# MoBA heads with stationary values and eight row buffers, difference heads with two steps scored early

## The reference

```
# MoBA (8 heads of 64): with 512 tokens and blocks of 256, the top-3 choice of earlier blocks
# takes every earlier block, so each head is causal softmax attention with a linear bias
s = q @ k.T * scale - slope * dist           # 128 rows x (128, 256, 384 or 512) keys per row tile
o = softmax(s) @ v
z = concatenate([o_nsa, o_moba]) @ w_out

# heads with differences (4 heads, two maps m of 64 each, values of 128), no causal mask
p = softmax(q_m @ k_m.T * scale - slope * |dist|)     # m = 0, 1
o = (p[0] - lam * p[1]) @ v
o = rms(o, subln) * 0.8 * silu(gate)
```

## Time and profile before

| | us |
|---|---|
| median of three runs | 1905.12 |
| profiled execution, device time | 1898.13 |
| its span | 1896.2 |
| PE busy in it | 1795.2 (95%) |
| DVE busy | 686.3 (36%) |
| ACT busy | 388.5 (20%) |

### The profile page before, as it was taken

How to read it: one execution, slowest core, us unless ns; L and a number is a source line. 1 busy time by engine, 2 the same in 40 slices (tenths; PEclk the granted TensorE clock), 3 DMA queues, 4 the chain that set the end, 5 groups by cost and what they waited for, 6 DMA issues and landing times.

```text
span 1896.2 us, 32235 instructions
## 1 busy us (share of the span) xinstructions
PE 1795.2 (95%) x13254; PEld 844.1 (45%) x13254; DVE 686.3 (36%) x1747; ACT 388.5 (20%) x910; POOL 139.2 (7%) x209
## 2 busy tenths in 40 slices
PE   5999999999999999999999989999999889989999
PEld 3567657746333332333233323333333274656854
DVE  3469775513223222232322213231313143296140
ACT  2127521602111111111111111011111022261110
POOL 2020000000010011001101101011010100000000
PEclk9999999997999999999999999999999999999999
DMA  9912231422999999999999999999999792100001
GB/s 322 296 45 90 90 107 47 185 78 100 338 386 395 402 405 400 405 387 401 399 402 401 401 404 399 405 390 388 406 402 414 291 309 67 45 1 1 1 0 45
DMA packets 133403, 495.25 MB, mean 261 GB/s; under 512 B 22587, under 2 KB 72677, under 8 KB 84104
## 3 DMA queue, kind: packets, MB, share of 16 engines
q1 hardware_dynamic: 116624, 466.91, 63.3%
q0 software_dynamic: 11264, 19.27, 4.3%
q10 hardware_dynamic: 5368, 7.00, 1.0%
HBM read 481.08 MB, written 17.43 MB: 263 GB/s over the span
## 4 chain that ended last, share of the span: by engine, by line
PE 69%; DMA 20%; DVE 7%; issue 2%; ACT 1%; SPq 1%; POOL 0%; ACTq 0%; DVEq 0%; POOLq 0%
PE bank L1593 22%; DMA ring<-in_exp_w_dram 18%; PE bank L1616 11%; PE bank L437 10%; PE bank L450 8%; PE bank L857 6%; DVE arena L720 2%; PE bank L639 1%; DVE arena L689 1%; DVE arena L805 1%; PE bank L1581 1%; PE bank L412 1%; DMA arena<-in_x_dram 1%; SPq L990 1%; PE bank L1566 1%
## 5 line engine op out<-in xcount | busy, mean ns | idle before, releaser
L1593 PE MATMUL bank<-ring,arena 128*32 128x512 f32 x5568 | 638.1, 599 | 28.4 <-DMA ring<-in_exp_w_dram 19.2
L1593 PEld LDWEIGHTS bank<-ring,arena 128*32 128x32 f32 x5568 | 170.2, 110 | 381.6 <-issue 329.9
L1616 PE MATMUL bank<-ring,arena 128*32 128x512 f32 (+1 forms) x3392 | 309.6, 518 | 16.9 <-DMA ring<-in_exp_w_dram 15.6
L1616 PEld LDWEIGHTS bank<-ring,arena 128*32 128x32 f32 x3392 | 109.7, 110 | 219.1 <-issue 172.5
L437 PE MATMUL bank<-hT,ring 128*128 128x512 f32 x448 | 201.5, 600 | 2.0 <-ACT hT L840 1.1
L1298 ACT ACTIVATE arena<-bank,mod,small 128x96 f32<-128x96 f32 (+2 forms) x256 | 87.4, 423 | 545.2 <-PE bank L1581 545.2
L2060 DVE COPY arena<-bank 128x8 f32<-128x8 f32 (+1 forms) x32 | 5.3, 164 | 363.1 <-PE bank L1566 353.2
L437 PEld LDWEIGHTS bank<-hT,ring 128*128 128x128 f32 x448 | 84.1, 191 | 101.3 <-issue 98.5
L450 PE MATMUL bank<-ring,hT 128*128 128x256 f32 (+1 forms) x640 | 128.2, 360 | 0.0
L2074 DVE TENSOR_TENSOR arena<-bank,arena 128x512 f32<-128x512 f32 x87 | 54.9, 683 | 189.1 <-PE bank L1593 189.1
L450 PEld LDWEIGHTS bank<-ring,hT 128*128 128x128 f32 x640 | 111.4, 190 | 15.2 <-issue 2.4
(11 more groups left out here) (405 smaller groups left out, 1517.6 us busy)
## 6 DMA issues: line engine op xcount, KB each, us to landing
ring<-in_exp_w_dram SPq DMA_DIRECT2D x384, 1024.0 KB, 27.5
ring<-in_ada_w_dram SPq DMA_DIRECT2D x24, 1024.0 KB, 11.8
ring<-in_w_in_dram SPq DMA_DIRECT2D x23, 1024.0 KB, 11.9
ring<-in_w_out_dram SPq DMA_DIRECT2D x8, 1024.0 KB, 5.1
arena<-in_x_dram ACTq DMA_DIRECT2D x1, 2048.0 KB, 17.2
ring<-in_w_in_dram SPq DMA_DIRECT2D x8, 256.0 KB, 5.1
expert_sums<-arena POOLq DMA_DIRECT2D x4, 512.0 KB, 4.2
h_rows<-arena ACTq DMA_DIRECT2D x4, 512.0 KB, 2.6
```

The costliest lines, as they stand in the source:

```text
L1593: mm = pe.matmul(bank[g][QUAD * c:QUAD * (c + 1), :].rearrange("p (h n) -> p h n", h=2), rowsT[:, k, QUAD * g:QUAD * (g + 1)], w[:, :, SW ...
L1616: mm = pe.matmul(bank[b][QUAD * c:QUAD * (c + 1), 0:width], rowsT[:, g, 2 * q + j, :], w[:, col:col + width], start=(q == 0 and j == 0), s ...
```

## The change

MoBA. Eight row buffers instead of three. The probabilities are divided by their row sum on DVE over the whole width before they are transposed. Both heads of a pair get a buffer of turned probabilities of their own (`pair_pT`, keys on partitions, all 512 queries along the row), which ACT fills step by step. When the eight steps of a pair of heads are turned, PE multiplies with 64 columns of values stationary and the turned probabilities moving, 512, 384, 256 and 128 columns wide, the two heads on the two halves of one bank. The result comes out with features on partitions, as `w_out` needs it, and DVE copies it to `hT` in one instruction. The transposes of the NSA half of `omix` move between the first MoBA scores; those of the MoBA half are gone. PE transposes three pairs behind the scores.

Heads with differences. The scores, minima and exps of the first two steps are placed behind the last gate job but one. The PSUM banks are dealt out anew so that this is possible. On DVE the second map gets the factor -lambda * sum0 / sum1 and is added to the unscaled first map; the division by sum0 is applied to the 128-wide result.

```diff
+        moba_p = [work[:, n, :] for n in range(4)] + [omix[:, n, 0:S] for n in range(4)]
+        pair_pT = [omix[:, :, 512:1024], room(6144, [NT, S])]
...
+        def pe_moba(pe):
...
+            def turn(st):
+                n = st["at"]
+                pe.wait_ge(p_ok, n - O_NSA + 1)
+                pe.wait_ge(t_ok, n - 1)
+                for b in range(st["blocks"]):
+                    mm = pe.transpose(bank[4 + n % 2][:, b * P:(b + 1) * P], st["p"][:, b * P:(b + 1) * P], ident[:, :])
+                mm.then_inc(t_done, 1)
+
+            def values(t):
+                pe.wait_ge(t_ok, O_NSA + PAIR * (t + 1))
+                if t >= 2:
+                    pe.wait_ge(o_acc, O_NSA + PAIR * (t - 1))
+                for b in range(NT):
+                    for h in range(2):
+                        lanes = slice(HD * h, HD * (h + 1))
+                        mm = pe.matmul(bank[6 + t % 2][lanes, P * b:S], vtok[:, b, P * t + HD * h:P * t + HD * (h + 1)],
+                                       pair_pT[h][:, b, P * b:S], start=(b == 0), stop=(b == NT - 1), skip_group_check=True)
+                mm.then_inc(o_done, PAIR)
+            pairs = len(moba_steps) // 2
+            for m in range(pairs + LATER):
+                if m < pairs:
+                    scores(moba_steps[2 * m], moba_steps[2 * m + 1])
+                if m < 2:
+                    mixed_turned(pe, 2 * m)
+                    mixed_turned(pe, 2 * m + 1)
+                if m >= LATER:
+                    turn(moba_steps[2 * (m - LATER)])
+                    turn(moba_steps[2 * (m - LATER) + 1])
+                    if m >= LATER + NT and (m - LATER) % NT == 0:
+                        values((m - LATER) // NT - 1)
+            values(pairs // NT - 1)
...
+            def copy(st):
+                n, i, k = st["at"], st["i"], st["at"] - O_NSA
+                act.wait_ge(t_done, n + 1)
+                if k >= PAIR:
+                    act.wait_ge(o_done, O_NSA + PAIR * (k // PAIR))
+                act.activation(pair_pT[st["half"]][:, 0:i + 1, P * i:P * (i + 1)],
+                               bank[4 + n % 2][:, 0:P * (i + 1)].rearrange("p (b q) -> p b q", q=P), ACT.Copy).then_inc(t_ok, 1)
...
+                if m in (0, 2):
+                    mixed(m)
+                    mixed(m + 1)
...
+            def over_sum(st):
...
+                dve.wait_ge(s_exp, n + 1)
+                link(dve.reciprocal(c, ls[:, n % 4:n % 4 + 1]))
+                dve.tensor_scalar(st["p"][:, 0:w], st["p"][:, 0:w], c, None, ALU.mult).then_inc(p_ok, 1)
+
+            def take(t):
+                dve.wait_ge(o_done, O_NSA + PAIR * (t + 1))
+                dve.tensor_copy(hT[:, 4 + t, :], bank[6 + t % 2][:, :]).then_inc(o_acc, PAIR)
...
-                link(dve.reciprocal(c, ls[:, n % 4:n % 4 + 2]))
-                dve.tensor_tensor(c[:, 1:2], lam[:, 5:6], c[:, 1:2], ALU.mult)
-                link(dve.tensor_scalar(p0, p0, c[:, 0:1], None, ALU.mult))
-                dve.scalar_tensor_tensor(out=p0, in0=p1, scalar=c[:, 1:2], in1=p0, op0=ALU.mult, op1=ALU.add)\
-                   .then_inc(w_ok, 1)
+                dve.reciprocal(over, ls[:, n % 4:n % 4 + 1])
+                link(dve.reciprocal(c, ls[:, n % 4 + 1:n % 4 + 2]))
+                link(dve.scalar_tensor_tensor(out=c, in0=c, scalar=lam[:, 5:6], in1=ls[:, n % 4:n % 4 + 1], op0=ALU.mult,
+                                              op1=ALU.mult))
+                dve.scalar_tensor_tensor(out=p0, in0=p1, scalar=c, in1=p0, op0=ALU.mult, op1=ALU.add).then_inc(w_ok, 1)
...
-                dve.tensor_copy(st["dst"], bank[6 + st["at"] % 2][:, 0:P]).then_inc(o_acc, 1)
+                dve.tensor_scalar(st["dst"], bank[1 + st["at"] % 2][:, 0:P], da_over[:, j % 4:j % 4 + 1], None, ALU.mult)\
+                   .then_inc(o_acc, 1)
...
+            act_project(act, link, da_jobs, {da_jobs[-2]["at"]: first_exps})
...
+            dve_project(dve, link, da_jobs, {da_values[1]["at"]: normed, da_jobs[-2]["at"]: first_minima})
```

More of the change, by code:

```diff
@@ L591, in two_block_layer @@
                     bias=bias8[:, h, S - P * (i + 1):S], blocks=i + 1,
-                    over=None, dst=omix[:, i, 512 + HD * h:512 + HD * h + HD], add=False))
+                    i=i, half=h % 2))
         for h in range(4):
@@ L726, in dve_attend, with mixed_turned @@
                     accumulate(steps[m - 3])
-        def pe_da(pe):
[L730 to L735, removed]
+        PAIR = 2 * NT
+        LATER = 3
+        def mixed_turned(pe, t):
+            if t >= 2:
+                pe.wait_ge(mixT_ok, t - 1)
+            for i in range(NT):
+                mm = pe.transpose(bank[6 + t % 2][:, i * P:(i + 1) * P], omix[:, i, t * P:(t + 1) * P], ident[:, :])
+            mm.then_inc(mixT_t, 1)
@@ new lines, in dve_moba @@
+        def dve_moba(dve, link):
+            def over_sum(st):
+                n, w = st["at"], P * st["blocks"]
+                c = cf[:, n % 4:n % 4 + 1]
+                dve.wait_ge(s_exp, n + 1)
[4 more added lines that the diff above has]
+                dve.tensor_copy(hT[:, 4 + t, :], bank[6 + t % 2][:, :]).then_inc(o_acc, PAIR)
+            for m in range(len(moba_steps) + 2):
+                if m < len(moba_steps):
+                    st = moba_steps[m]
+                    n, w = st["at"], P * st["blocks"]
+                    dve.wait_ge(s_done, n + 1)
+                    if m >= 4:
+                        dve.wait_ge(s_exp, n - 3)
+                    if m == 4:
+                        dve.wait_ge(mixT_t, 4)
+                    if m >= 8:
+                        dve.wait_ge(t_done, n - 7)
+                    dve.tensor_tensor_reduce(out=st["p"][:, 0:w], in0=bank[n % 4][:, 0:w], in1=st["bias"],
+                                             scale=1.0, scalar=3e38, op0=ALU.add, op1=ALU.min,
+                                             accum_out=mn[:, n % 4:n % 4 + 1]).then_inc(s_bias, 1)
+                if m >= 2:
+                    over_sum(moba_steps[m - 2])
+                if m >= 2 * PAIR - 1 and (m + 1) % PAIR == 0:
+                    take((m + 1) // PAIR - 2)
+            take(len(moba_steps) // PAIR - 1)
@@ L737, in turn, with da_scores @@
+        DA_BANK = (3, 4, 5, 6)
+        def da_scores(pe, st):
+            for m in range(2):
+                n = O_MOBA + 2 * (st["at"] - O_MOBA) + m
+                if n >= O_MOBA + 4:
+                    pe.wait_ge(s_bias, n - 3)
+                pe.matmul(bank[DA_BANK[n % 4]][:, :], st["q"][m], st["k"][m], start=True, stop=True).then_inc(s_done, 1)
+        def pe_da(pe):
             def turn(st):
@@ L843, in pe_out @@
         def pe_out(pe, r, name, res0):
[L844 to L850 removed]
+            pe.wait_ge(mixT_ok, 4 + ND * r)
             for n in range(ND):
```

126 lines of the change are left out of this document (75 added, 51 removed).

## The result

The changed kernel takes 1890.75 us, the median of seven runs (1888.65 to 1896.85); the kernel before, run beside it, 1903.03 (seven runs, 1899.61 to 1905.35). The ratio is 0.9943 with a 95% interval of 0.9932 to 0.9955, so the change brings 10.9 us (8.6 to 12.9). The forecast was 1890.5, from a gain of 14.5 us. The time came out on the forecast and the gain did not: the median of the kernel before was 2.1 us lower over these seven runs than over the three of them that the forecast started from, and the stages gained less than the sum said.

The account below looks back on a forecast made before the run. PE was taken to bound MoBA, DVE the difference heads, DMA the experts. Gains of 9.0 (MoBA) and 5.5 (differences) sum to 14.5 us: 1905.1 - 14.5 = 1890.6, written 1890.5; range 1884 to 1901.

Parts of the forecast that it names:

- The bound of the stages: PE bounds MoBA and w_out, DVE the difference heads, DMA the experts; gains in MoBA and difference heads add.
- Values side by side: MoBA: both heads' value products run together on PE, 2.4 us for a pair.
- Rival 2: MoBA: values don't run side by side; MoBA -0.6 us, differences 5.5, total 1900.2; chance 0.10.
- The count of eight more changes: MoBA on PE: eight more tiling mode changes at 0.1 us each, 0.8 us longer, left out of the sum.
- PE's work in a group: MoBA, eight steps: scores 2.98, transposes 2.6, values 2.4, sum 8.0 us.
- The coupling: MoBA: ACT's first copy of the next pair waits 2.0 us for the values, giving 9.1 us a group.
- The start: MoBA from its first score: DVE sets the pace after exp 2, first pair done at 16.8 us.
- Rival 4: PE falls to its lower clock; all of MoBA at half clock adds 26 us, total 1916.6; chance 0.06.
- The tail: MoBA's end: last exp, divisions, transposes, copies, values 2.5 and copy to hT 0.7; w_out 42.0 us after first score.
- The differences: Difference heads: steps 2.65 instead of 2.87 us, start 2.2 us earlier; gain 5.5 us, bounds 3.5 and 6.5.
- Rival 1: MoBA: coupling tighter, groups 10.2 us, start and tail 2 us more; MoBA gains 3.7, total 9.2, 1895.9; chance 0.18.
- Rivals 2 and 3: Rival 3, difference heads: PE and DVE wait for each other, step 2.85, nearly only the start gains; 1893.6; chance 0.08.

Follow-up runs that it names:

- the hold: The changed kernel plus two 512-column products with unread results in PE's pause before the transposes of step 2; 1889.88 us, one run.
- copies by block: The changed kernel, but each copy of turned probabilities waits only for value products of the key blocks it overwrites; 1894.83 us, ratio to before 0.9954.
- the kernel with the differences alone: The changed kernel with MoBA's buffers and functions as before, so only the difference heads are changed; 1897.90 us, ratio to before 0.9973.

## Why the prediction came out, step by step

- **The bound of the stages: right in the main.** PE stays the busiest engine of a MoBA group (8.70 of 9.78 us), but a group is 1.1 us longer than its work; DVE stays the bound of the differences. The gains of the two places add.
- **Values side by side: right.** 2.4 us forecast, 2.38 measured. Rival 2 would have needed 4.8. They come out at the rate of the experts' quarters, 1.86 us for 1000 columns per head against 1.88.
- The Trainium skill (TensorEngine Tiling, Key Properties) says that a change of the tiling mode drains the engine. No run here separates such a drain from what else a short piece costs. The count of eight more changes was too high: by the order of PE's stream the values stand three times between transposes and scores, where one change was before, and once between transposes and w_out, which makes five. Splitting the values makes eight pieces more of them, and the records of all value products then add up to 11.3 us instead of 9.5: some 0.2 us a piece, start and end included.
- **PE's work in a group: mis-sized**, 8.0 against 8.70. Counted from the start of each piece to the next, or to its end where PE then idles, the values take 2.3 us (2.4 in the sum) and the scores 0.49 + 0.64 + 0.84 + 1.06 = 3.0 (2.98). The term that was wrong is the transposes, 3.4 instead of 2.6: two of them in a piece take 0.41 and one 0.30, where 0.13 each was taken from a piece of three.
- **The coupling: the step that failed.** The prediction held ACT's wait for the single buffer (2.0 us; measured 1.7) to set the group at 9.1. Measured 9.77. Cutting that wait to 0.54 us changed no group, nor did taking DVE's away. With both eased the group was 9.88. What the prediction left out is the order on PE: values in one piece keep the next scores back, DVE runs out of work, and the time is not made up. Splitting them brought groups of 9.03 and 9.35, which shows this for 0.4 to 0.7 us of a group. What part of the rest belongs to two banks of turned blocks and what to a lag that ends where DVE's division begins was not separated.
- **The start: off by 2.0 us** (first pair done after 18.8, forecast 16.8). Rival 4 had the mechanism, with the chance of a disaster and no term in the sum. The clock fell for some 4 us only, and cost 1.6; with the hold it is 17.3, within 0.5 of the forecast.
- **The tail: off by 1.1 us** (8.1 from the third pair's values to w_out, forecast 7.0). There the single buffer does count: copies by block give 7.2.
- These three and the two groups (2 x 0.67) are 4.4 us, and 42.0 + 4.4 = 46.4 is the stage of 46.50. A part of the 51.0 of before was itself a fallen clock: the old MoBA in the kernel with the differences alone had none and took 49.68. Without a fall on either side the gain is 49.68 - 44.93 = 4.75 us.
- **The differences: right to 0.2 us in each term.** Steps of 2.65 us. Below, one step of the kernel after, which answers to the earlier trace rows.

```profile
1680.38 0.16 DVE L922 RECIPROCAL small<-ls 128x1 f32<-128x1 f32 x1
1680.46 0.14 DVE L923 RECIPROCAL cf<-ls 128x1 f32<-128x1 f32 x1
1680.64 0.22 DVE L924 SCALAR_TENSOR_TENSOR cf<-cf,small,ls 128x1 f32<-128x1 f32 x1
1680.89 0.75 DVE L926 SCALAR_TENSOR_TENSOR arena<-arena,cf 128x512 f32<-128x512 f32 x1
1681.56 0.34 DVE L931 TENSOR_SCALAR arena<-bank,small 128x128 f32<-128x128 f32 x1
1681.70 0.66 PE L863 MATMUL bank<-ident,arena 128*128 128x128 f32 x4
1681.82 0.68 DVE L910 CUSTOM_DVE_ANT_0 arena<-bank,arena 128x512 f32<-128x512 f32 x1
```

In this step DVE has no gap, and PE no wait in front of L863 where it waited 0.27. L922 comes again at 1683.04, 2.66 later. L924 is 0.22 us (0.20 with its wait was taken, bounds 0.08 and 0.3). Where the differences begin, which answers to the earlier trace rows:

```profile
1661.74 1.13 PE L854 MATMUL bank<-arena 64*128 64x512 f32 x4 [1.26 <-DVE arena L576]
...
1664.64 0.75 DVE L926 SCALAR_TENSOR_TENSOR arena<-arena,cf 128x512 f32<-128x512 f32 x1
```

The second difference ends at 1664.64 + 0.75 = 1665.39, 21.4 us after the third-last job's end (L488 at 1643.98); before it was 1667.26, 23.5 us after the same instruction (1643.79). That is 2.1 us for the start (2.2 forecast). From there to retention it is 39.3 us instead of 42.7: 3.4 us for the steps and the last difference (3.2 forecast).

- **The rivals.** Rival 1, tighter coupling, given 0.18, had a gain of 3.7 us in MoBA and 9.2 in all. The stages gained 4.5 and 9.9: nearer to it than to the forecast's 9.0 and 14.5, with groups of 9.8 instead of 10.2. Rivals 2 and 3 did not come. That the time was met to 0.3 us is luck, because errors cancelled: 4.6 us too much gain in the stages, a start 2.1 us too high, and a difference of the medians (12.3 us) above what ratio and stages say.

## What to carry over

Ask of a long piece of work on the busiest engine not only how long it is, but what it keeps back behind it: the stock in front of the other engines (here the scores of one step) must last as long as the piece, or the piece is to be cut. Here cutting it gave 0.4 to 0.7 us of a group of 9.8. A wait seen in the profile is a candidate, not a cause; two waits of 1.7 and 0.9 us were eased here and the groups gained nothing, because another stood behind each. Add the granted clock at a stage's start to the sum as a term, whenever PE waits there more than before.

## What the runs showed of the hardware

Two 64-column halves of float32 products, each with moving columns of its own, run fully side by side: 16 records in 2.37 us, as many columns per time as four 32-column quarters. The granted clock fell to 0.50 (1.2 GHz) behind pauses of 1.68 and 0.72 us early in MoBA, and did not with two products, 2 us of work, laid into the first of them. Three table loads on ACT around the last gate job took 1.28 us each, and ACT waited for PE or DVE behind the second and the third:

```profile
1651.96 1.28 ACT L889 ACT_TABLE_LOAD   x1
...
1656.25 1.28 ACT L552 ACT_TABLE_LOAD   x1
1660.36 0.60 ACT L552 ACTIVATE arena<-bank 128x512 f32<-128x512 f32 x1 [2.83 <-PE bank L458]
1660.98 1.28 ACT L1485 ACT_TABLE_LOAD   x1
```
